# Norms and modulation sums of a two-block model: squares in a PSUM bank, scale prepared at the seventh tile, two blocks a tile, one group behind the centering

## What is computed

```python
def rmsnorm(x, g):
    xf = x.astype(jnp.float32)
    y = xf * lax.rsqrt(jnp.mean(xf * xf, axis=-1, keepdims=True) + EPS)
    return (y * g.astype(jnp.float32)).astype(x.dtype)
...
        mod = c_act @ w_ada[i] + b_ada[i]
        sh1, sc1, g1, sh2, sc2, g2 = jnp.split(mod, 6, axis=-1)
        h = modulate(rmsnorm(x, norm_mix_g[i]), sh1, sc1)
...
        x = x + g1[:, None, :] * m
```

## Time and profile before

| | |
|---|---|
| median of 3 runs (lowest, highest) | 1711.39 us (1711.31, 1717.99) |
| the profiled execution, its own time | 1714.21 us |
| its span, first to last instruction | 1712.4 us, mean granted TensorE clock 0.989 |
| TensorE matmuls busy | 1652.0 us (96% of the span) |
| TensorE weight loads busy | 1334.1 us (78%) |
| VectorE busy | 859.5 us (50%) |
| ScalarE busy | 582.8 us (34%) |
| GpSimd busy | 735.2 us (43%) |
| traffic | 233.71 MB, mean 136 GB/s |

### The profile page before, as it was taken

One profiled execution on the slowest core, in us unless ns is written; L12 is line 12 of the kernel. 1 busy time (PEld: TensorE's weight loads), 2 busy tenths in 40 slices (PEclk: granted clock), 3 DMA queues, 4 the chain that ended last, 5 costly groups with the idle time before them and its releaser, 6 DMA issues.

```text
span 1712.4 us, 21074 instructions
## 1 busy us (share of the span) xinstructions
PE 1652.0 (96%) x7260; PEld 1334.1 (78%) x7260; DVE 859.5 (50%) x1255; ACT 582.8 (34%) x794; POOL 735.2 (43%) x342
## 2 busy tenths in 40 slices
PE   8999898998999999999999999999999999999997
PEld 6785677777877888888878878788887788888886
DVE  6899887878576333433375181551717311111114
ACT  5434342243524322222243342332433432222233
POOL 4899132453244444444444233233323344444442
PEclk9999999999999999999999999999999999999998
DMA  9352264375366554555442222122212232222221
GB/s 375 110 199 64 79 233 174 131 241 204 125 234 227 197 199 175 191 197 183 168 168 88 83 87 95 64 81 78 86 60 74 74 98 98 98 98 99 88 75 59
DMA packets 65442, 233.71 MB, mean 136 GB/s; under 512 B 7264, under 2 KB 7264, under 8 KB 65120
## 3 DMA queue, kind: packets, MB, share of 16 engines
q1 hardware_dynamic: 65376, 232.82, 38.9%
HBM read 230.69 MB, written 2.10 MB: 136 GB/s over the span
## 4 chain that ended last, share of the span: by engine, by line
issue 61%; POOL 31%; PE 4%; DVE 2%; ACT 1%; POOLq 1%; DMA 0%; ACTq 0%; DVEq 0%
POOL w_lo L468 27%; POOL cv_acc L511 2%; PE bank L1442 1%; PE bank L1443 1%; PE bank L1444 1%; POOL diag L505 1%; POOL sq L505 1%; PE ps_stat L1505 0%; POOL cv_y L493 0%; DVE mods_ring L1050 0%; DVE cv_acc L1050 0%; POOLq L467 0%; POOL h_lo L534 0%; POOLq L537 0%; PE c_all L1544 0%
## 5 line engine op out<-in xcount | busy, mean ns | idle before, releaser
L468 POOL TENSOR_TENSOR w_lo<-w_raw,w_hi 128x1024 fp32r<-128x1024 f32 x268 | 652.9, 2441 | 923.7 <-ACT w_hi L552 907.4
L1442 PE MATMUL bank<-h_hi,w_hi 128*128 128x512 f32 x1240 | 488.5, 394 | 14.8 <-POOL w_lo L468 12.2
L1444 PE MATMUL bank<-h_hi,w_lo 128*128 128x512 f32 x1240 | 485.1, 391 | 0.0
L1443 PE MATMUL bank<-h_lo,w_hi 128*128 128x512 f32 x1240 | 485.1, 391 | 0.0
L552 ACT ACTIVATE w_hi<-w_raw 128x1024 fp32r<-128x1024 f32 x264 | 277.7, 1052 | 234.4 <-PE bank L1444 219.8
L1442 PEld LDWEIGHTS bank<-h_hi,w_hi 128*128 128x128 f32 x1240 | 234.2, 189 | 67.0 <-POOL w_lo L468 14.3
L1443 PEld LDWEIGHTS bank<-h_lo,w_hi 128*128 128x128 f32 x1240 | 234.4, 189 | 49.7 <-issue 1.0
L1444 PEld LDWEIGHTS bank<-h_hi,w_lo 128*128 128x128 f32 x1240 | 234.2, 189 | 49.3
L1442 PE MATMUL bank<-f_hi,w_hi 128*128 128x512 f32 x472 | 185.3, 393 | 5.2 <-POOL w_lo L468 5.2
L1443 PE MATMUL bank<-f_lo,w_hi 128*128 128x512 f32 x472 | 185.0, 392 | 0.0
L1287 DVE TENSOR_TENSOR z_buf<-bank,s_buf 128x512 f32<-128x512 f32 x44 | 30.4, 692 | 306.2 <-PE bank L1444 306.2
(11 more groups left out here) (234 smaller groups left out, 1949.8 us busy)
## 6 DMA issues: line engine op xcount, KB each, us to landing
mods_ring<-w_mods_in SPq DMA_DIRECT2D x152, 512.0 KB, 5.9
w_raw<-ff_in_in SPq DMA_DIRECT2D x88, 512.0 KB, 3.5
w_raw<-ret_in SPq DMA_DIRECT2D x64, 512.0 KB, 3.5
w_raw<-ff_out_in SPq DMA_DIRECT2D x32, 512.0 KB, 3.5
w_raw<-cv_ab_in SPq DMA_DIRECT2D x16, 512.0 KB, 5.7
w_raw<-ff_tail_in SPq DMA_DIRECT2D x16, 384.0 KB, 3.0
w_raw<-cv_g_in SPq DMA_DIRECT2D x8, 512.0 KB, 3.5
w_raw<-cv_out_in SPq DMA_DIRECT2D x8, 512.0 KB, 3.5
```

Of the source, the lines that this page charges most:

```text
L468: pool.tensor_tensor(w_lo[:, s, :], w_raw[:, s, :], w_hi[:, s, :].bitcast(F32), ALU.subtract).then_inc(lo_done, 1)
L1442: pe.matmul(out, w_h, m_h, start=start, stop=False)
L1443: pe.matmul(out, w_h, m_l, start=False, stop=False)
L1444: return pe.matmul(out, w_l, m_h, start=False, stop=stop)
```

## The change

Six edits, of which the diff shows all:

- The running sum of squares of n1, n3, n4, n5 and n6 lies in the PSUM bank `ps_bc`, and the seventh addition writes it to `ssum`.
- `prepare` is called in `out` before the addition x6, no more at the head of `norm`.
- In `out` the modulation blocks come two before each of the first tiles, where four came before each of half as many.
- Group 5 of the modulation, which was summed whole ahead of the centering, has one block there and three behind it; group 6, of which three blocks were behind the centering, is summed whole ahead of `cv_out`.
- Group 22 is summed behind norm 3 and no more in `fr_out`.
- `stat` has one filler matmul of 256 columns between the two column sums; the filler behind them has 384 columns instead of 512.

```diff
-BUSY = {"std": 1, "norm": 2, "conv": 6, "squares": 3, "layer norm": 4, "first norm": 4}
+BUSY = {"std": 1, "last square": 1, "norm": 2, "conv": 6, "squares": 3, "layer norm": 4, "first norm": 4}
...
-                so_far = ps_stat if stat in AHEAD else ssum
+                so_far = ps_stat if stat in AHEAD else ssum if stat[0] == "h" else ps_bc
                 if c == 0:
                     v.tensor_copy(so_far[:], sq[:]).then_inc(sum_step, 1)
                 else:
-                    v.tensor_tensor((so_far if c < DC - 1 else ssum)[:], so_far[:], sq[:],
+                    last = DC - 1 if stat in AHEAD else DC - 2
+                    v.tensor_tensor((so_far if c < last else ssum)[:], so_far[:], sq[:],
                                     ALU.add).then_inc(sum_step, 1)
...
             def norm(n, stat, lo=True):
 
-                if STATS[stat] not in AHEAD:
-                    prepare(n)
                 inverse(stat)
...
                 for j in range(DC):
-                    if g is not None and j < upto:
-                        sum_mods(g + j)
-                    if ahead is not None and j == first and stat != "n2":
+                    if g is not None and j < 2 * upto:
+                        sum_blocks(g + j // 2, (2 * (j % 2), 2 * (j % 2) + 1))
+                        if j % 2:
+                            end_mods(g + j // 2)
+                    if stat is not None and ahead is None and j == DC - 2:
                         prepare(int(stat[1]))
...
-            sum_mods(5)
-            add_bias(SHIFT[0] + 2 * DC, DC)
+            sum_blocks(5, (0,))
             v.wait_ge(mean_done, 1)
...
-            sum_blocks(6, (0, 1))
+            sum_blocks(5, (1, 2))
             inverse(ST["cv"])
-            sum_blocks(6, (2,))
+            sum_blocks(5, (3,))
...
+            end_mods(5)
+            add_bias(SHIFT[0] + 2 * DC, DC)
             v.wait_ge(mod_step, steps["mod"])
-            sum_blocks(6, (3,))
-            end_mods(6)
+            sum_mods(6)
             out("cv_out", 0, "n1", g=7, upto=3)
...
-            out("fr_out", 2, "n3", g=19, upto=4)
+            out("fr_out", 2, "n3", g=19, upto=3)
+            norm(3, ST["n3"])
+            sum_mods(22)
             g = 23
-            norm(3, ST["n3"])
...
-            def keep_busy(n, out):
+            def keep_busy(n, out, width=T):
 
 
                 for _ in range(n):
-                    pe.matmul(out[:], ones[:], vec[:, 0:T], start=True, stop=True)
+                    pe.matmul(out[:, 0:width], ones[:], vec[:, 0:width], start=True, stop=True)
...
                 columns(ssum, True, False)
+                keep_busy(BUSY["last square"], ps_bc, T // 2)
                 pe.wait_ge(sq_ready, SQ0[name] + DC)
                 columns(sq, False, True).then_inc(stat_done, 1)
-                keep_busy(BUSY["std"], ps_bc)
+                keep_busy(BUSY["std"], ps_bc, 3 * P)
```

## The result

The changed kernel takes 1721.62 us (median of 7 runs, 1717.44 to 1723.50), the kernel before 1711.62 us (7 runs, 1709.45 to 1717.99): a ratio of 1.0049 with a 95% interval of 1.0034 to 1.0064. It is 8 us slower by the ratio and 10 by the medians, where I forecast 9 us faster. The profiled execution took 1718.64 us, its span 1716.9.

A forecast was written before the change was run, and what follows sets the result against it. TensorE, busy 96% of the span, was taken as the bound. Terms of -5.6 and -4.5 of clock made -10.1 from the profiled 1714.2, so 1704.1; 1.6 off for the lower median gave 1702.5 us, range 1695 to 1709.

The forecast's parts named there:

- Centering: At the centering: VectorE starts earlier, TensorE's wait for the pair sums goes, -2.7 us; the clock there, -1.7.
- `pl_out`: In `pl_out`: the wait at 423.45 goes, but VectorE becomes the bound; -0.4 us, bounds -1.5 and +0.5.
- The sums in PSUM: Running sums at the norms cost 0.70 instead of 1.10 us, reaching the path only on last tiles: -0.2 in n5.
- The fifth unit behind norm 3: Behind norm 3: the next projection's fifth unit loads only after group 22's blocks; +1.8 us, bounds 0 and +2.5.
- rival 4: `cv_out`, `fr_out`, behind norm 3: weight units load behind later modulation blocks, holding ScalarE's casts; 1716 us, chance 0.05.
- rival 3: At n1, n3, n4 and n5: `prepare` is held, 6.8 us instead of 0.6, less 2; 1707 us, chance 0.07.
- my four signs of being wrong: Centering no earlier than about 184; DMA-released casts in `fr_out`; bias row over 1 us; norms over 7 us, low clocks.
- `prepare`: Ahead of x6 at the norms: may meet a GpSimd subtraction and delay x6 and x7; +0.6 us, bounds 0 and 6.8.
- `cv_out`: In `cv_out`: two waits for units go, the unit behind x0 becomes late; -1.8 us, bounds -2.8 and 0.
- The first SwiGLU: In its last part, before n4: the wait of 1.16 us at 870.87 goes; -1.0, between -1.16 and -0.2.
- The clock at the norms: At n1, n5 and n6: the filler between column sums recovers half of 5.7 us; -2.8, bounds 0 and -5.7.
- the fillers: At five norms: the shortened filler lets the spreading start 0.2 us earlier; -1.0 us in all.

The follow-up runs named there:

- e4: The kernel before with the centering edit alone (one block of group 5 ahead, three behind, group 6 whole ahead of `cv_out`): 1710.37 us, ratio 0.9986.
- e12: e10 with the running sums of the squares back in SBUF: 1705.39 us, ratio 0.9959 to the kernel before.
- e3: The changed kernel with the first SwiGLU's first four weight units loaded ahead of group 22 and `prepare` back behind x7 in the norm: 1711.35 us.
- e1: The changed kernel with the first SwiGLU's first four weight units loaded ahead of group 22's blocks: 1711.95 us, ratio 0.9995 to the kernel before.
- e6: e3 with all four groups in `fr_out`, none behind norm 3, loads of group 22 and the SwiGLU's first units interleaved: 1713.78 us.
- e2: The changed kernel with `prepare` back in the norm, behind x7: 1717.17 us, ratio 1.0022 to the kernel before.
- e9: The kernel before with `prepare` moved ahead of x6 alone: 1715.44 us, ratio 1.0026.
- e11: The changed kernel with four blocks a tile again in the SwiGLU's projections alone: 1716.80 us, ratio 1.0034 to the kernel before.
- e7: The kernel before with TensorE's fillers alone changed (256 columns between the column sums, 384 instead of 512 behind): 1710.41 us, ratio 0.9998.
- e8: e5 and e6 together, with the filler behind the column sums back at 512 columns: 1715.04 us, ratio 1.0015 to the kernel before.
- e5: e3 with two blocks a tile in `cv_out` starting at the second tile, first `pl_v` units loaded between and ahead of group 9's blocks: 1713.19 us.
- e10: The changed kernel with `prepare` back in the norm, group 22 back in `fr_out`, four blocks a tile in `fr_out` and the SwiGLU: 1705.95 us.

## Why the prediction was wrong

Right, by their own steps:
- Centering (-2.7, and -1.7 of clock): e4's stage shows 4.5. In the changed kernel TensorE is 3.45 us ahead at 215.68 (219.13 before), since a clock fall came at the channel sum (0.55 in 178.6 to 182.1).
- `pl_out`: the wait at 423.45 went, and VectorE became the bound as I had said; TensorE waits 0.90 us for its last addition at 429.35, so 0.65 is left of the 1.55.
- The sums in PSUM: 0.70 us, and worth next to nothing (e12).
- The fifth unit behind norm 3: +1.8 forecast within 0 to 2.5, measured 2.59 (changed kernel), 2.99 (e3) and 3.41 us (e1). The mechanism was right: e6, with nothing behind the norm, has no such wait. The size was short: the fifth unit's load left at 539.14, 1.2 us behind group 22's last block (537.93), and its cast began at 545.10, 6.0 us later, where I had added 3.5 to 5.9 to the end of the block.

Wrong:
1. **"It decides when the load behind group 9 or 22 lands later than the sixth square; by my count it is 0 to 2 us earlier at `fr_out`."** This is the step that failed, and rival 4 was the case that came, with a chance of 0.05. The measured 1721.6 lies just above rival 4's own range (1712 to 1721): rival 3's held `prepare` came with it, and I had priced each alone. Three of my four signs of being wrong were there: a cast in `fr_out` released by a DMA, the bias row at over 1 us ahead of x6, norms of 8.5 and 10.0 us.

   The count could not have come out so. Group 21's last block stands directly ahead of x5's addition: the load left at 499.78 and x5's addition was done at 499.92, so x5 was ready to be squared 0.14 us after the issue, and a load takes far longer than that (the median is 3.5 us; this one took 6.1). The first unit's cast stands in ScalarE's order ahead of that square. I had counted load and square in old times by two different chains, though one block releases both.

   It cost 7.19 us of waiting (3.6 of them `prepare`, held as a result), and a norm at the lower clock behind it, 10.0 us instead of 6.5; e1 took 9.7 us away. My size for it, 4 to 5 us at `fr_out`, was a little high without `prepare` (3.55 in e2). At `cv_out` nothing of the kind happened, because the four units there stand behind the loads of group 9, which group 8's blocks ahead of x3 release: the first left at 243.20, two tiles ahead of x5, and its cast waited 0.50 us. At `fr_out` the group in that place of the queue is 22, whose blocks VectorE does only behind norm 3, and its loads are released by group 21's blocks ahead of x4 and x5.
2. **`prepare`, +0.6 with 0 to 6.8.** e9 measures 4.4 (1.9 to 7.2). My reason for the low end was that the earlier additions take the queue of casts away. They don't: the additions behind the last blocks come 2.05 us apart, a subtraction takes 2.4, so GpSimd works without a break exactly at x6. The trace of before had this, in a row of GpSimd's timeline at n4 that I had not used:

```profile
868.45 16.41 POOL L468 TENSOR_TENSOR w_lo<-w_raw,w_hi 128x1024 fp32r<-128x1024 f32 x6 [4.12 <-ACT w_hi L552]
```

   Rival 3 was the reading to take: its 6.8 less 2 is 4.8, near e9's 4.4. The rule of the Trainium skill (SBUF — State Buffer, "Who interferes with whom"), by which a VectorE instruction with two SBUF inputs and a GpSimd instruction that reads SBUF lock each other out, pointed at it, and the runs agree: each of the two instructions was held for up to 2.4 us, about a whole subtraction, where GpSimd was busy (e3, e9, e11), and took 0.17 where it wasn't (e1 at n3). I had also priced one held instruction; it is two, and the second can be held for longer than the first.
3. **`cv_out`, -1.8 within -2.8 and 0.** The unit behind x0 was 2.16 us late, not 0.7, as data of group 7 made VectorE wait (0.97 us), and a wait of 0.94 at n1 stands there too. Two waits of 2.83 in all went and 3.10 came: about 0, the bound that I had named for just this cause. The stage's 1.1 us less lies in n1, where the way from the column sums to the spreading took 2.97 us instead of 4.21 (clock and shorter filler). The two blocks a tile did pay here all the same: with the old grouping behind the new centering the wait is e4's 5.55 us.
4. **The first SwiGLU, -1.0.** The wait for the unit did go, and the late x4 to x6 with the held `prepare` put 2.39 us and a clock fall in its place; e11 gives the sum, 4.8 us between the medians.
5. **The clock at the norms, -2.8, and the fillers, -1.0.** e7 measures both as 0.3 us faster, with an interval of 2.6 faster to 1.9 slower. That n1 kept its clock after the change means little: it did so in e4 with the old fillers, and fell in e7 with the new. I had read one execution's draw there as a property of a norm; at n5 it may be one (e7 above). What did repeat is that a wait of 2.0 to 7.3 us ahead of a norm's column sums was followed by a fall, ten times of ten (n3 after and in e2, e6, e8, e9 and e11; n4 after and in e1; n1 in e5 and e8). With the longer of these waits the warning of the Trainium skill (TensorE: Matmul & The Clock Gate, "Why this matters for your kernels") against idle gaps agrees; for the norms without such a wait, some of which fell too (n3 in e1, n4 in e10, n1 in e3, e7 and e10), no run here shows what decides.

By the measured steps, against before: centering -4.5 and `cv_out` 0, n3 +7.2 and +3.5 of clock, less 1.4 for the waits of `pl_out` and `fr_out` (1.55 - 0.90 and 0.72), behind norm 3 +2.6, n4 +2.4 less 0.9 (1.16 - 0.29) and +2.2 of clock: +11.1. The medians differ by 10.0. All but the centering is read from one profile of each kernel, so a closer agreement would be luck.

Left open: what decides a clock fall at a norm without a wait; whether the filler keeps the clock at n5; whether e8's three edits would pay if the modulation of group 22 had a place outside both `fr_out` and the SwiGLU, which wasn't tried.

## What to carry to other kernels

Before moving work that frees a buffer, write down what is loaded behind that buffer in the same queue, and which instruction of an in-order engine stands first in line for it: if the block that releases the load is also the last thing ahead of the work whose result waits behind it, nearly the whole load is a wait, whatever the times were before. A small instruction is free only in a place where the engine that can hold it is idle, so ask for that engine's row at the new place; and before counting a clock fall as a cost of its place, see whether a second execution has it there.

## What the runs showed of the hardware

- Two small VectorE instructions of 0.17 us each (128x16 and 128x8) took up to 2.37 us (e9) and 2.33 us (e11) while GpSimd subtracted, at times both in a row, each to the end of another subtraction (1.30 and 2.25 us after). The 128x4 copies of the modulation sums took up to 1.87 us instead of 0.17, again to the end of a subtraction (e3: until 504.20, where the subtraction ends at 504.17).
- Four 512 KB loads issued within 2.5 us behind modulation loads (499.78 after) landed 6.1 to 8.0 us after their issue, where the median of this stream is 3.5.
- Single executions of the kernel before differ by over 10 us (1706.2 to 1719.2), with mean granted clocks of 0.983 to 0.994 that tend to be lower in the longer ones, and that is more than any edit here was worth; so a profile's own time (e5's 1719.5 beside a median of 1713.2) says little of an edit, and the waits in it say more.
